# Ten expert blocks on chip instead of nine, gathered tokens and result rows in one buffer each, and a scatter by column halves

## The chip, the core and the metric

The kernel runs on one core of a Trainium2 chip. The metric is the device time of one execution in microseconds; lower is better. All work is float32. Engines are named as in the profile: PE (TensorE matmul), PEld (its weight loads), DVE (VectorE), ACT (ScalarE), POOL (GpSimd), SP (SyncE, which issues nearly all loads).

## What is computed

Two layers of a hybrid encoder block on 256 tokens of width 1024. Each layer has a mixer (one wide input projection, differential attention, a bidirectional state-space scan, gates, output projections) and then a hierarchical mixture of experts, in which each token goes to two of 32 experts:

```python
for i in range(DEPTH):                        # 2
    h = rms_norm(x, norm1_g[i])
    q, k, v, z, xbc, dt_raw, gate_a, gate_m = split(h @ w_in[i])
    ya = diff_attention(q, k, v, lam, rel_bias) @ w_attn_out[i]
    ym = ssd_mixer(z, xbc, dt_raw, ...) @ w_ssm_out[i]
    x = x + (sigmoid(gate_a) * ya + sigmoid(gate_m) * ym) @ w_out[i]
    hn = rms_norm(x, norm2_g[i])
    x = x + hier_moe(hn, ...)                 # top group of 4, top 2 of its 8 experts
# one expert: (silu(xb @ w_gate[e]) * (xb @ w_up[e])) @ w_down[e], 1024 -> 512 -> 1024
```

## The kernel before

Each engine has its own program; they meet at semaphores. A table of PSUM fills, `mixer_fills`, fixes in which order each of the eight PSUM banks is filled; `full`, `free`, `out_of` and `before` are waits on the counters of that table, `fill` and `drain` raise them.

**Mixer.** Weights come in 28 blocks of 2 MB through a ring of three slots (0 to 2). ACT copies each chunk of a block to a rounded high part (`cast`, L1324; four chunks of staging, `high`, in slot 3), POOL makes the low part (L2160), and PE multiplies in three products per tile (L791 to L793). SP issues the block loads in order (L645), each when the block three before it has been used (`BLOCK_USE`).

**Expert pass** (`first_pass`). All 32 experts are computed in 16 pairs; each expert takes up to 64 tokens, so a pair fills the 128 columns or rows of the array, one expert per half. Expert weights are 96 blocks of 2 MB in each layer: per pair two gate, two up and two down blocks, in that order. They go through nine slots (`slot_at`), in the order `ORDER`; load n is issued when block n - SLOTS has been used (`used`, L622). The first nine loads are issued by hand in the last part of the mixer as the memory under each slot comes free; loads 9 to 12 go in quarters and halves (L631), and so do the last pair's up and down blocks. Slots overlap mixer buffers: slot 6 is `r_h` and `r_g`, slot 7 `r_bt`, slot 8 `r_q` and `r_k`, slot 3 the staging of the high parts.

For one pair j, PE does: gate product g and up product u (L1185, 32 records of 7 us each), the scatter of pair j-1 for the first token half (`scatter`, L1130 and L1131), part of the gather for the pair of pairs after (`gather`, L1145: half of the work in every pair), the transposes of the hidden units (L1199), the turned selection matrix G (L1205, L1207), the scatter of the second token half, and the down product y2 in two column halves (L1217). ACT does silu (L1595), the copy of the hidden units (L1602), the copy of G (L1608, L1612), and the high rows of the result (L1619); DVE does the product of gate and up (L2053), the adds into X (L2061) and the low rows (L2071). Gathered tokens have two buffers (`xgT2`), result rows two column halves each for high and low (`yeh`, `yel`). The scatter of pair j runs in pair j+1; that of the last pair stands at the end, and after it either the next layer's norm (ACT L1342) or the store of the output (SP L747).

## Time and profile before

| | us |
|---|---|
| median of three runs | 1781.48 |
| lowest and highest | 1781.36, 1782.14 |
| profiled execution | 1784.47 |
| its span, first to last instruction | 1782.5 |
| PE busy | 1696.4 (95%) |
| DVE, ACT, POOL busy | 743.6, 684.7, 667.8 |
| loads and stores | 528.47 MB, 296 GB/s over the span |
| first expert product, layer 0 and layer 1 | 447.65 and 1332.89 |

Busy is time with an instruction on the engine. A matmul's end is modelled, so short waits inside a run of matmuls do not show as idle; a wait that the profile can't put down to another engine's instruction is called "issue". A DMA has its issue on SP, 0.33 us, and a time to landing; what counts for the reader of a slot is the landing.

### The profile page before, as it was taken

The numbers are of one execution on the slowest core, as the hardware profiler recorded it, in microseconds if no ns is written. First come the engines' busy times: TensorE is split into PE (matmuls) and PEld (weight loads), VectorE is DVE, ScalarE is ACT, GpSimd is POOL, SyncE is SP. The second block draws the span as 40 slices with busy tenths as digits, with TensorE's granted clock in tenths as the row PEclk, the third lists the DMA queues.
The fourth block names the chain that finished last, engine by engine and source line by source line (L and its number), as shares of the span: only waits on it lengthen the run. The fifth ranks groups of instructions, "written<-read, shape, count | busy, mean of one in ns | idle before, by whom it ended". The sixth has DMA issues, their size and how long they took to land.

```text
span 1782.5 us, 23201 instructions
## 1 busy us (share of the span) xinstructions
PE 1696.4 (95%) x8978; PEld 1057.9 (59%) x8978; DVE 743.6 (42%) x1318; ACT 684.7 (38%) x1541; POOL 667.8 (37%) x536
## 2 busy tenths in 40 slices
PE   8999999999999998999999999999999999998988
PEld 5889877776434434343368898777764444343433
DVE  5728787634222222211166387867341122121212
ACT  4565787744211111111056667877441111111111
POOL 6888776884000000000067987778830000000000
PEclk9999999999999999999999999999999999999999
DMA  6554312466999999999944452215669999999997
GB/s 250 206 189 154 131 58 86 151 252 281 418 419 427 427 429 427 427 427 428 415 193 171 184 189 95 96 48 194 267 281 416 428 427 428 429 427 427 428 428 302
DMA packets 45795, 528.47 MB, mean 296 GB/s; under 512 B 4936, under 2 KB 7752, under 8 KB 14960
## 3 DMA queue, kind: packets, MB, share of 16 engines
q1 hardware_dynamic: 45648, 526.89, 72.0%
q8 instruction: 76, 1.25, 0.3%
q14 instruction: 39, 0.32, 0.1%
q0 software_dynamic: 32, 0.02, 0.0%
HBM read 525.82 MB, written 1.06 MB: 296 GB/s over the span
## 4 chain that ended last, share of the span: by engine, by line
PE 77%; DVE 15%; issue 4%; ACT 3%; POOL 0%; DMA 0%; SPq 0%; DVEq 0%; ACTq 0%
PE PS L1185 25%; PE PS L1217 13%; PE PS L791 8%; PE PS L793 7%; PE PS L792 7%; DVE view L1807 5%; PE PS L1145 3%; PE PS L1130 3%; PE PS L1131 2%; DVE view L1803 1%; PE PS L998 1%; DVE view L1995 1%; DVE view L2061 1%; ACT view L1436 1%; PE PS L779 1%
## 5 line engine op out<-in xcount | busy, mean ns | idle before, releaser
L2160 POOL TENSOR_TENSOR view<-view,view 128x512 fp32r<-128x512 f32 x448 | 579.4, 1319 | 574.3 <-DVE view L1709 477.6
L1185 PE MATMUL PS<-view,view 128*64 128x512 f32 x2048 | 456.7, 602 | 35.1 <-issue 34.5
L1185 PEld LDWEIGHTS PS<-view,view 128*64 128x64 f32 x2048 | 157.7, 139 | 328.4 <-issue 328.1
L1324 ACT ACTIVATE view<-view 128x512 fp32r<-128x512 f32 x448 | 273.4, 629 | 155.7 <-PE PS L793 145.6
L791 PE MATMUL PS<-view,view 128*128 128x512 f32 x704 | 285.9, 406 | 5.7 <-POOL view L2160 3.2
L792 PE MATMUL PS<-view,view 128*128 128x512 f32 x704 | 275.4, 391 | 0.0
L793 PE MATMUL PS<-view,view 128*128 128x512 f32 x704 | 275.4, 391 | 0.0
L1217 PE MATMUL PS<-view,stb 128*64 128x512 f32 x1024 | 226.8, 595 | 0.3
L2053 DVE TENSOR_TENSOR view<-PS,view 128x512 f32<-128x512 f32 x32 | 22.1, 692 | 421.7 <-PE PS L1185 421.7
L791 PEld LDWEIGHTS PS<-view,view 128*128 128x128 f32 x704 | 132.6, 188 | 35.4 <-issue 7.5
L1217 PEld LDWEIGHTS PS<-view,stb 128*64 128x64 f32 x1024 | 70.7, 137 | 139.3 <-issue 138.8
L793 PEld LDWEIGHTS PS<-view,view 128*128 128x128 f32 x704 | 132.6, 188 | 29.2
L792 PEld LDWEIGHTS PS<-view,view 128*128 128x128 f32 x704 | 132.9, 189 | 23.4
L1560 ACT ACTIVATE view<-PS,vcol 128x256 f32<-128x256 f32 x64 | 26.7, 472 | 281.6 <-PE PS L1145 265.0
L2071 DVE SCALAR_TENSOR_TENSOR view<-PS,gcol,view 128x512 fp32r<-128x512 f32 x64 | 48.0, 751 | 205.5 <-ACT view L1619 205.5
L1619 ACT ACTIVATE view<-PS,gcol 128x512 fp32r<-128x512 f32 x64 | 44.0, 687 | 182.3 <-PE PS L1217 182.1
L896 PE MATMUL PS<-view,view 128*128 128x256 f32 x384 | 112.0, 292 | 0.0
L897 PE MATMUL PS<-view,view 128*128 128x256 f32 x384 | 108.6, 283 | 0.0
L898 PE MATMUL PS<-view,view 128*128 128x256 f32 x384 | 108.5, 282 | 0.0
L1595 ACT ACTIVATE view<-PS 128x512 f32<-128x512 f32 x32 | 19.1, 597 | 199.1 <-PE PS L1185 199.1
L1807 DVE SCALAR_TENSOR_TENSOR view<-PS,vcol,view 128x254 f32<-128x254 f32 x192 | 92.7, 483 | 6.8
L2061 DVE TENSOR_TENSOR view<-PS,view 128x512 f32<-128x512 f32 x128 | 82.6, 684 | 11.1 <-PE PS L1131 10.5
(250 smaller groups left out, 2038.1 us busy)
## 6 DMA issues: line engine op xcount, KB each, us to landing
view<-in_w_exp_gate_dram SPq DMA_DIRECT2D x62, 2048.0 KB, 27.9
view<-in_w_exp_up_dram SPq DMA_DIRECT2D x58, 2048.0 KB, 28.4
view<-in_w_mix_dram SPq DMA_DIRECT2D x56, 2048.0 KB, 7.8
view<-in_w_exp_down_dram SPq DMA_DIRECT2D x56, 2048.0 KB, 30.4
view<-in_w_exp_up_dram SPq DMA_DIRECT2D x24, 512.0 KB, 23.7
view<-in_w_exp_down_dram SPq DMA_DIRECT2D x24, 512.0 KB, 14.5
view<-in_w_exp_down_dram SPq DMA_DIRECT2D x4, 1024.0 KB, 10.6
view<-in_w_exp_gate_dram SPq DMA_DIRECT2D x4, 1024.0 KB, 13.0
```

Source lines behind the costliest of these rows:

```text
L791: pe.matmul(o, xh[:, k, ts], highs(chunk), start=(k == 0), stop=False)
L792: pe.matmul(o, xh[:, k, ts], weights(low8, chunk), start=False, stop=False)
L793: ins = pe.matmul(o, xl[:, k, ts], highs(chunk), start=False, stop=(k == last))
L896: pe.matmul(o, wh[:, i, :], hTh[:, k, :], start=(k == 0), stop=False)
L897: pe.matmul(o, wh[:, i, :], hTl[:, k, :], start=False, stop=False)
L898: ins = pe.matmul(o, wl[:, i, :], hTh[:, k, :], start=False, stop=(k == KD - 1))
L1185: ins = pe.matmul(bank(ph, name, j)[e * CAP:(e + 1) * CAP, :], xgT2[h % 2][:, k, at + e * CAP:at + (e + 1) * CAP], slot8[expert_block(j, k ...
L1217: ins = pe.matmul(PS[e * CAP:(e + 1) * CAP, 3 + n, :], hhT[:, k, e * CAP:(e + 1) * CAP], slot4[expert_block(j, 2, e)[1]][:, k, n * COLS:(n ...
L1324: nc.scalar.activation(highs(chunk), weights(slot8, chunk), ACT.Copy).then_inc(*high_ready.up(ph))
L1807: ins = v.scalar_tensor_tensor(out=a[:, lo:hi], in0=x_[:, lo + o:hi + o], scalar=w(j), in1=a[:, lo:hi], op0=ALU.mult, op1=ALU.add)
L2061: v.tensor_tensor(x_, bank(ph, "s", j, t, n), x_, ALU.add).then_inc(*drain(ph, "s", j, t, n))
L2160: g_.tensor_tensor(weights(low8, chunk), weights(slot8, chunk), highs(chunk), ALU.subtract).then_inc(*low_ready.up(ph))
```

## The change

- SLOTS goes from 9 to 10 with a new ORDER. The tenth slot is made of three pieces of memory (2048, 1024 and 1024 words of each partition), so a load of it is three DMAs.
- The room: gathered tokens get one buffer (`xgT1`), result rows one column half each for high and low (`yh`, `yl`; the very last half has a buffer of its own, `yh_end`, `yl_end`). Several mixer buffers move, and the high parts of the last mixer blocks are staged in `high2`.
- SP issues the first expert loads earlier and in another order: one after the scan, two around the gates, then one after another with the merging products; all ten before the expert pass. Two mixer blocks are loaded when their slot's own block has been used, not one block later. The next layer's first three mixer blocks wait for the second-last down product; the dt weights (`step_weights`) wait for the last scatter.
- The scatter goes by column halves (`put_back`): half 0 of pair j-1 after g of pair j, half 1 after u. The gather for the next two pairs stands wholly in odd pairs, in four parts. In the last pair both scatters and G stand between g and u.

```diff
-SLOTS = 9
+SLOTS = 10
 RING = 3
-ORDER = (4, 5, 1, 2, 7, 8, 0, 3, 6)
+ORDER = (7, 3, 6, 4, 5, 8, 1, 2, 0, 9)
+PIECES = ((0, 2048), (2048, 1024), (3072, 1024))
...
 def gathered(j):
 
-    return (2 * (j % 2), 2 * (j % 2) + 1) if j // 2 + 1 < HALVES else ()
+    return j % 2 == 1 and j // 2 + 1 < HALVES
...
-        f += [(("g", j), 0), (("u", j), 1)]
+        f.append((("g", j), 0))
         if j:
-            f += [(("s", j - 1, 0, n), 5 + n) for n in range(2)]
-        f += [(("xg", j // 2 + 1, i), 4 if i % 2 else 7) for i in gathered(j)]
+            f += [(("s", j - 1, t, 0), 5 + t) for t in range(TT)]
+        if j == ALL_PAIRS - 1:
+            f.append((("G", j), 7))
+            f += [(("s", j - 1, t, 1), 5 + t) for t in range(TT)]
+            f.append((("u", j), 1))
+        else:
+            f.append((("u", j), 1))
+            if j:
+                f += [(("s", j - 1, t, 1), 5 + t) for t in range(TT)]
+        if gathered(j):
+            f.append((("xg", j // 2 + 1, 0), 0))
         f.append((("hh", j), 2))
-        if j:
-            f += [(("s", j - 1, 1, n), 5 + n) for n in range(2)]
-        f.append((("G", j), 7))
-        f += [(("y2", j, n), 3 + n) for n in range(2)]
-    f += [(("s", ALL_PAIRS - 1, t, n), 5 + n) for t in range(TT) for n in range(2)]
+        if j < ALL_PAIRS - 1:
+            f.append((("G", j), 7))
+        if gathered(j):
+            f.append((("xg", j // 2 + 1, 1), 1))
+        f.append((("y2", j, 0), 3))
+        if gathered(j):
+            f.append((("xg", j // 2 + 1, 2), 7))
+        f.append((("y2", j, 1), 4))
+        if gathered(j):
+            f.append((("xg", j // 2 + 1, 3), 2))
+    f += [(("s", ALL_PAIRS - 1, t, 0), 5 + t) for t in range(TT)]
+    f += [(("s", ALL_PAIRS - 1, t, 1), t) for t in range(TT)]
...
+        xgT1 = view(r_x, KD, HALF)
+        yh, yl = (view(r_v + i * COLS, COLS, dt=F32R) for i in range(2))
+        yh_end, yl_end = (view(r_x + i * COLS, COLS, dt=F32R) for i in range(2))
...
-        sga, sgm = ([view(r + o, TT, COLS) for r in (r_g, r_w)] for o in (0, 1024))
-        junk = view(r_v, 2 * D)
+        ga0, gm0 = (view(r_g + i * 1024, TT, COLS) for i in range(2))
+        sga, sgm = ([view(r + n * 1024, TT, COLS) for n in range(2)] for r in (r_v, r_w))
+        junk = view(r_q, 2 * D)
...
-        S2 = [view(r, TT, HALF, dt=F32R) for r in (r_cbt + TT * P, r_rt)]
+        high2 = view(r_cbt, HIGHS, COLS, dt=F32R)
+        pieces = (r_x + 2 * D, r_v + D, r_cbt)
...
-            h = high[:, chunk % HIGHS, :]
+            h = (high2 if chunk >= REST + HIGHS else high)[:, chunk % HIGHS, :]
...
+                    if slot == SLOTS - 1:
+                        for to, (at, width) in zip(piece4 if kind == 2 else piece8, PIECES):
+                            sp.dma_start(to.rearrange("p k f -> p (k f)"), src.rearrange("a p f -> p (a f)")[:, at:at + width]
+                                         ).then_inc(*loaded[slot].up(ph))
+                        return
...
-                        sp.wait_ge(*filled[0 if i else 1].at(ph, 0))
+                        if l:
+                            sp.wait_ge(*filled[4].at(ph, -1))
+                    elif i - RING in (FB + 5, FB + 7):
+                        sp.wait_ge(*chunk_used.at(ph, CHUNK_USE[(i - RING + 1) * CHUNKS - 1]))
                     else:
                         sp.wait_ge(*full(ph, *BLOCK_USE[i - RING]))
                     sp.dma_start(slot8[i % RING].rearrange("p k c -> p (k c)"), src).then_inc(*loaded[i % RING].up(ph))
                     if l == 0 and i == RING - 1:
                         vectors(0, ph)
+                        step_weights(0, ph)
+                    if l and i == RING - 1:
+
+                        sp.wait_ge(*full(Phase(l - 1), "s", ALL_PAIRS - 1, 1, 1))
+                        step_weights(l, ph)
                     if i == RING + 1:
 
                         sp.wait_ge(*filled[4].at(ph, 0))
                         sp.wait_ge(s_skew, 16)
                         sp.dma_start(BT, bass.AP(table_dram.tensor, 0, [[1, P], [WIN, HEADS], [1, 384]])
                                      ).then_inc(*bt_in.up(ph))
+                    if i == FB + 5:
+
+                        sp.wait_ge(*out_of(ph, "sc", ATT - 1))
+                        sp.wait_ge(*full(ph, "y", UNITS_SCAN - 1))
+                        load(0, 0, 0)
                     if i == FB + 7:
+
+                        sp.wait_ge(*full(ph, "gm", 1, 1))
+                        load(0, 0, 1)
+                        sp.wait_ge(*gate_ready.at(ph, 2))
+                        load(0, 1, 0)
+                    if i == FB + 8:
 
                         sp.wait_ge(*full(ph, "mT", XT - 1))
                         sp.wait_ge(*sumsq.at(ph, 13))
-                        load(0, 0, 0)
+                        load(0, 1, 1)
                     if i == FB + 11:
 
                         sp.wait_ge(*full(ph, "ws", 1, 1))
-                        load(0, 0, 1)
                         load(0, 2, 0)
                 sp.wait_ge(*full(ph, "wa", 1, 1))
-                load(0, 1, 0)
-                sp.wait_ge(*full(ph, "wo", 0, 1))
-                load(0, 1, 1)
-                sp.wait_ge(*full(ph, "wo", 1, 1))
                 load(0, 2, 1)
                 load(1, 0, 0)
+                sp.wait_ge(*full(ph, "wo", 0, 1))
                 load(1, 0, 1)
-                sp.wait_ge(*full(ph, "lgT"))
+                sp.wait_ge(*full(ph, "wo", 1, 1))
                 load(1, 1, 0)
+                load(1, 1, 1)
...
+            def put_back(ph, j, n):
+
+                high_rows, low_rows = (yh_end, yl_end) if j == ALL_PAIRS - 1 and n else (yh, yl)
+                pe.wait_ge(*out_of(ph, "y2", j, n))
+                if n == 0:
+                    pe.wait_ge(*out_of(ph, "G", j))
+                for t in range(TT):
+                    pe.wait_ge(*free(ph, "s", j, t, n))
+                    o, pick_t = bank(ph, "s", j, t, n), Gm[:, t * P:(t + 1) * P]
+                    pe.matmul(o, pick_t, high_rows, start=True, stop=False)
+                    pe.matmul(o, pick_t, low_rows, start=False, stop=True).then_inc(*fill(ph, "s", j, t, n))
...
+                        if kind == 0:
+                            if j:
+                                put_back(ph, j - 1, 0)
+                            if j == ALL_PAIRS - 1:
+                                turned_selection(j)
+                                put_back(ph, j - 1, 1)
+                    if 0 < j < ALL_PAIRS - 1:
+                        put_back(ph, j - 1, 1)
+                    if gathered(j):
+                        gather(h + 1, 0)
                     pe.wait_ge(*out_of(ph, "u", j))
                     pe.wait_ge(*free(ph, "hh", j))
                     for k in range(FF // P):
                         ins = pe.transpose(PS[:, 2, k * P:(k + 1) * P], hh[:, k * P:(k + 1) * P], ident[:, :])
                     ins.then_inc(*fill(ph, "hh", j))
-                    if j == 0:
-                        pe.wait_ge(*gw_ready.at(ph, 1))
-                    pe.wait_ge(*free(ph, "G", j))
-                    for t in range(TT):
-                        pe.transpose(PS[:, 7, t * P:(t + 1) * P], S2[h % 2][:, t, at:at + P].bitcast(F32), ident[:, :])
-                    for t in range(TT):
-                        ins = pe.matmul(PS[:, 7, TT * P:TT * P + 2], S2[h % 2][:, t, at:at + P].bitcast(F32),
-                                        gw[:, t, 2 * j:2 * j + 2],
-                                        start=(t == 0), stop=(t == TT - 1))
-                    ins.then_inc(*fill(ph, "G", j))
-                    if j:
-                        scatter(ph, j - 1, 1)
+                    if j < ALL_PAIRS - 1:
+                        turned_selection(j)
+                    if gathered(j):
+                        gather(h + 1, 1)
                     pe.wait_ge(*out_of(ph, "hh", j))
...
+                                gather(h + 1, 2 + n)
...
-                for t in range(TT):
-                    scatter(ph, ALL_PAIRS - 1, t)
+                for n in range(2):
+                    put_back(ph, ALL_PAIRS - 1, n)
...
-                    for i in gathered(j):
-                        if i % 2 == 0:
-                            gathered_out(j // 2 + 1, i)
-                    rest(ph, j)
+                    if j:
+                        high_rows(ph, j - 1, 1)
+                    if j == ALL_PAIRS - 1:
+                        selection_out(ph, j)
+                    hidden_out(ph, j)
+                    if j < ALL_PAIRS - 1:
+                        selection_out(ph, j)
+                    if gathered(j):
+                        gathered_out(j // 2 + 1, 0)
+                    high_rows(ph, j, 0)
+                    if gathered(j):
+                        gathered_out(j // 2 + 1, 2)
                     if j == 2:
                         act.wait_ge(*flag_ready.at(ph, 1))
                         act.sem_inc(s_anchor, 1)
                         over = act.value_load(flag[0:1, 0:1], min_val=0, max_val=1)
+                high_rows(ph, ALL_PAIRS - 1, 1)
...
+            def high_rows(ph, j, n):
+
+                act.wait_ge(*full(ph, "y2", j, n))
+                end = j == ALL_PAIRS - 1 and n
+                if n and not end:
+                    act.wait_ge(*full(ph, "s", j, 1, 0))
+                elif j and not end:
+                    act.wait_ge(*full(ph, "s", j - 1, 1, 1))
+                nc.scalar.activation(yh_end if end else yh, PS[:, 3 + n, :], ACT.Copy, scale=gcol[:, 0:1]
+                                     ).then_inc(*yeh_ready.up(ph))
...
+                    if j:
+                        low_rows(ph, j - 1, 1)
+                        add(ph, j - 1, 0)
                     if j % 2 == 0 and j // 2 + 1 < HALVES:
                         select(j // 2 + 1)
+                    if j == ALL_PAIRS - 1:
+                        add(ph, j - 1, 1)
                     gated(ph, j)
-                    for i in gathered(j):
-                        if i % 2:
-                            gathered_out(j // 2 + 1, i)
-                    if j:
-                        add(ph, j - 1)
-                    scaled_low(ph, j)
+                    if 0 < j < ALL_PAIRS - 1:
+                        add(ph, j - 1, 1)
+                    if gathered(j):
+                        gathered_out(j // 2 + 1, 1)
+                    low_rows(ph, j, 0)
+                    if gathered(j):
+                        gathered_out(j // 2 + 1, 3)
                     if j == 2:
                         dve.wait_ge(*flag_ready.at(ph, 1))
                         dve.sem_inc(s_anchor, 1)
                         over = dve.value_load(flag[0:1, 0:1], min_val=0, max_val=1)
                     if j == ALL_PAIRS // 2 and l + 1 < DEPTH:
                         head_scales(Phase(l + 1))
-                add(ph, ALL_PAIRS - 1)
+                low_rows(ph, ALL_PAIRS - 1, 1)
+                for n in range(2):
+                    add(ph, ALL_PAIRS - 1, n)
```

## Rows read from the trace of the kernel before

**Rows 1.** Page, part 2: what the DMA engines moved in each fortieth of the span

```profile
GB/s 250 206 189 154 131 58 86 151 252 281 418 419 427 427 429 427 427 427 428 415 193 171 184 189 95 96 48 194 267 281 416 428 427 428 429 427 427 428 428 302
```

**Rows 2.** Windows, layer 0: us, busy per engine, clock, DMA share, GB/s; second: 512 KB loads

```profile
540.00:580.00 40.00, 38.68 (x200) 17.67 (x200) 10.57 (x19) 7.42 (x17) 0.00 (x0) 1.00 1.01 428
...
872.00:877.00 5.00, 5.00 (x26) 1.73 (x24) 0.00 (x0) 0.60 (x1) 0.00 (x0) 1.00 1.03 410
```

**Rows 3.** Timeline of PE: start, us, work; layer 0 to pair 2, layer 1 start

```profile
447.65 13.96 PE L1185 MATMUL PS<-view,view 128*64 128x512 f32 x64 [0.30 <-ACT view L1560]
461.53 2.17 PE L1145 MATMUL PS<-view,view 128*128 128x256 f32 x16
...
471.75 13.90 PE L1185 MATMUL PS<-view,view 128*64 128x512 f32 x64
...
490.34 0.47 PE L1130 MATMUL PS<-view,view 128*128 128x512 f32 x1 [0.66 <-DVE view L2061]
...
498.49 13.90 PE L1185 MATMUL PS<-view,view 128*64 128x512 f32 x64
...
1332.89 13.95 PE L1185 MATMUL PS<-view,view 128*64 128x512 f32 x64 [0.31 <-ACT view L1560]
```

**Rows 4.** Timeline of SP's DMA issues, layer 0: start, us from first to last issue

```profile
353.92 28.93 SPq L645 DMA_DIRECT2D view<-in_w_mix_dram  x4
...
431.74 0.33 SPq L622 DMA_DIRECT2D view<-in_w_exp_down_dram  x1
...
449.62 0.33 SPq L631 DMA_DIRECT2D view<-in_w_exp_up_dram  x1
...
472.33 6.82 SPq L622 DMA_DIRECT2D view<-in_w_exp_up_dram  x2
```

**Rows 5.** DMA view, us to landing, issued 417.45, 471.96, 472.33, 838.36, 1357.20

```profile
view<-in_w_exp_up_dram SPq DMA_DIRECT2D x1, 2048.0 KB, 7.7
...
view<-in_w_exp_gate_dram SPq DMA_DIRECT2D x1, 2048.0 KB, 9.1
...
view<-in_w_exp_up_dram SPq DMA_DIRECT2D x1, 2048.0 KB, 13.6
...
view<-in_w_exp_gate_dram SPq DMA_DIRECT2D x1, 2048.0 KB, 28.7
...
view<-in_w_exp_gate_dram SPq DMA_DIRECT2D x1, 2048.0 KB, 8.5
```

**Rows 6.** Timeline of PE, late pairs: products behind a wait; last two: last pairs

```profile
730.12 8.78 PE L1185 MATMUL PS<-view,view 128*64 128x512 f32 x32 [2.41 <-issue]
...
847.58 7.09 PE L1185 MATMUL PS<-view,view 128*64 128x512 f32 x32 [2.40 <-issue]
...
867.18 15.60 PE L1185 MATMUL PS<-view,view 128*64 128x512 f32 x64 [2.34 <-issue]
...
1749.90 13.95 PE L1185 MATMUL PS<-view,view 128*64 128x512 f32 x64 [0.64 <-issue]
```

**Rows 7.** Timeline of all engines, layer 0, behind the last pair's up product

```profile
882.82 0.69 DVE L2053 TENSOR_TENSOR view<-PS,view 128x512 f32<-128x512 f32 x1 [16.39 <-PE PS L1185]
...
884.39 0.60 ACT L1602 ACTIVATE stb<-PS 128x512 f32<-128x512 f32 x1 [7.84 <-PE PS L1199]
...
885.89 7.09 PE L1217 MATMUL PS<-view,stb 128*64 128x512 f32 x32
...
892.23 1.49 ACT L1619 ACTIVATE view<-PS,gcol 128x512 fp32r<-128x512 f32 x2 [5.57 <-PE PS L1217]
...
893.05 1.52 DVE L2071 SCALAR_TENSOR_TENSOR view<-PS,gcol,view 128x512 fp32r<-128x512 f32 x2 [6.23 <-ACT view L1619]
...
893.85 0.50 PE L1130 MATMUL PS<-view,view 128*128 128x512 f32 x1 [0.88 <-DVE view L2071]
...
894.62 3.03 DVE L2061 TENSOR_TENSOR view<-PS,view 128x512 f32<-128x512 f32 x4
```

**Rows 8.** Timeline of PE in the mixer of layer 0, second scan projection

```profile
364.21 0.44 PE L779 MATMUL PS<-ident,view 128*128 128x128 f32 x2 [2.52 <-DVE view L1700]
```

More of the change, by code:

```diff
@@ L407, in encoder @@
         small = sb("small", [P, 48])
[L408 removed]
         dtv, av, nac, eac, dend = (dtm[:, i] for i in range(5))
+        piece8 = [view(at, n // COLS, COLS) for at, (_, n) in zip(pieces, PIECES)]
+        piece4 = [view(at, n // D, D) for at, (_, n) in zip(pieces, PIECES)]
         ebias = av
@@ L1170, in first_pass, with turned_selection @@
                     first_gather(i, 1, XNl).then_inc(*fill(ph, "xg", 0, i))
+                def turned_selection(j):
+                    h, at = j // 2, (j % 2) * 2 * CAP
+                    if j == 0:
+                        pe.wait_ge(*gw_ready.at(ph, 1))
+                    pe.wait_ge(*free(ph, "G", j))
+                    for t in range(TT):
+                        pe.transpose(PS[:, 7, t * P:(t + 1) * P], S2[h % 2][:, t, at:at + P].bitcast(F32), ident[:, :])
+                    for t in range(TT):
+                        ins = pe.matmul(PS[:, 7, TT * P:TT * P + 2], S2[h % 2][:, t, at:at + P].bitcast(F32),
+                                        gw[:, t, 2 * j:2 * j + 2],
+                                        start=(t == 0), stop=(t == TT - 1))
+                    ins.then_inc(*fill(ph, "G", j))
                 for j in range(ALL_PAIRS):
@@ L1595, in gate, with hidden_out, selection_out @@
                 nc.scalar.activation(silug, PS[:, 0, :], ACT.Silu).then_inc(*drain(ph, "g", j))
+            def hidden_out(ph, j):
+                act.wait_ge(*full(ph, "hh", j))
+                act.wait_ge(*before(ph, "y2", j, 1))
+                nc.scalar.activation(hhT.rearrange("p k t -> p (k t)"), PS[:, 2, :], ACT.Copy
+                                     ).then_inc(*drain(ph, "hh", j))
+            def selection_out(ph, j):
+                act.wait_ge(*full(ph, "G", j))
+                if j:
+                    act.wait_ge(*full(ph, "s", j - 1, 1, 1))
+                act.wait_ge(*free(ph, "y2", j, 1))
+                nc.scalar.activation(Gm, PS[:, 7, 0:TT * P], ACT.Copy)
+                for e in range(2):
+                    rows = slice(e * CAP, (e + 1) * CAP)
+                    ins = nc.scalar.activation(gcol[rows, :], PS[rows, 7, TT * P + e:TT * P + e + 1], ACT.Copy)
+                ins.then_inc(*drain(ph, "G", j))
+                act.wait_ge(*out_of(ph, "G", j))
+            def high_rows(ph, j, n):
[4 more added lines that the diff above has]
+                elif j and not end:
+                    act.wait_ge(*full(ph, "s", j - 1, 1, 1))
+                nc.scalar.activation(yh_end if end else yh, PS[:, 3 + n, :], ACT.Copy, scale=gcol[:, 0:1]
+                                     ).then_inc(*yeh_ready.up(ph))
             def rest(ph, j):
-                yeh_done = yeh_ready if ph.unit is None else over_yeh[ph.layer]
                 act.wait_ge(*full(ph, "hh", j))
@@ L2053, in gated, with add, low_rows @@
                 v.tensor_tensor(hh, PS[:, 1, :], silug, ALU.mult).then_inc(*drain(ph, "u", j))
-            def add(ph, j):
+            def add(ph, j, n):
                 for t in range(TT):
-                    for n in range(2):
-                        x_ = X[:, t, n * COLS:(n + 1) * COLS]
-                        dve.wait_ge(*full(ph, "s", j, t, n))
-                        v.tensor_tensor(x_, bank(ph, "s", j, t, n), x_, ALU.add
-                                        ).then_inc(*drain(ph, "s", j, t, n))
+                    x_ = X[:, t, n * COLS:(n + 1) * COLS]
+                    dve.wait_ge(*full(ph, "s", j, t, n))
+                    v.tensor_tensor(x_, bank(ph, "s", j, t, n), x_, ALU.add
+                                    ).then_inc(*drain(ph, "s", j, t, n))
+            def low_rows(ph, j, n):
+                end = j == ALL_PAIRS - 1 and n
+                dve.wait_ge(*out_of(ph, "G", j))
+                dve.wait_ge(*yeh_ready.at(ph, 2 * j + n + 1))
+                v.scalar_tensor_tensor(out=yl_end if end else yl, in0=PS[:, 3 + n, :], scalar=gcol[:, 0:1],
+                                       in1=yh_end if end else yh, op0=ALU.mult, op1=ALU.subtract
+                                       ).then_inc(*drain(ph, "y2", j, n))
             def scaled_low(ph, j):
-                yeh_done = yeh_ready if ph.unit is None else over_yeh[ph.layer]
                 dve.wait_ge(*out_of(ph, "G", j))
```

93 lines of the change are left out of this document (52 added, 41 removed).

## Prediction

> **What bounds the kernel now.** I read the page's 40 slices first. From slice 11 to 19 and again from 31 to 39 the load rate stands at 418 to 429 GB/s, while the mixer before each stretch moves 58 to 281 GB/s [rows 1]. Those stretches are the expert passes: 96 loads of 2.10 MB in each layer. A window inside one says the same with the shares: PE 38.7 of 40 us, DMA share 1.01, 428 GB/s [rows 2]. At that rate one load takes 4.9 us and a pair of experts, six loads, 29.4 us. The timeline of PE gives the other side: pair 1 starts at 471.75 and pair 2 at 498.49 [rows 3], 26.7 us later and with no load waited for. So PE is faster than the queue, uses up its lead of nine slots and then has to wait. The late pairs show it: a wait of 2.3 to 2.4 us ahead of a product, named "issue", which is where a load lands [rows 6]. The landing of the second gate block of the last pair proves the tie: issued at 838.36, it lands 28.7 us later, at 867.06 [rows 5], and PE starts at 867.18 [rows 6]. In layer 1 the same product starts at 1749.90. So each layer is: time at which the last pair's gate blocks land, and then a chain of PE, ACT and DVE to the end. Both terms are changed here, with opposite signs.
>
> **Loads ahead: the gain.** Before, five loads are out when the last merging product ends; the other four of the nine slots are issued at 431.74 and after [rows 4]. After, eight of ten are out by then, and two more leave at once: 9.8 us plus about 2.8 us of latency (a lone load takes 7.7 us [rows 5], against 4.9 in the stream), so all ten are in by about 444, ahead of the first expert product at 447.65 [rows 3]. That empties the queue until the first quarter is released at 449.62 [rows 4], so three more slots are not worth three times 4.9 us. What counts is when load 14 (counted from 0, second load of the group released by pair 0's down product) lands. Before: issued 472.33, 13.6 us, so 485.9, or 38.3 us after the start of the expert pass [rows 3, 4, 5]. After: pair 0's down product ends earlier, because the gather between up and down (2.17 us [rows 3]) moves to pair 1. The gap from up to down, 24.1 less two products of 7.0 and one of 6.9, was 3.3 us with the gather in it and becomes 2.25 (the chain through the hidden units, worked out below), so that product ends at 23.0 us instead of 24.1. Load 14 is the first that it releases, the quarters ahead of it (four loads from 2.0 us on, 20 us) are just through, so it lands as a lone load, 7.7 us on, at 30.7 us. Lead: 7.6 us. In layer 1 the load before it is issued at 1357.20 and lands 8.5 us on, 32.8 us after that layer's start at 1332.89, where layer 0 needs 33.4 [rows 3, 5]; lead 7.0. From there both kernels run at the queue's rate and the lead stays: 14.6 us together. Ends: one slot each, 9.8; and 17 us if the queue keeps going.
> The cover for the lead is queue depth. Pair 1's down product releases the next loads at 49.2 us (23.0 + 7.0 gate + 0.9 + 7.0 up + about 11.3 for scatter, two gathers, hidden units, selection and down), and load 19 lands at 30.7 + 5 x 4.9 = 55.2, so 6 us of work remains and a gap needs less than 2.8.
>
> **Three pieces for slot 9: a cost.** Half of the tenth slot is loaded in pieces with rows of 4 KB. Where such loads run alone the window gives 410 GB/s against 428 [rows 2]: 1.05 MB takes 2.56 instead of 2.45 us. The 8 KB half has no row; I bound it between nothing and the same. Eight loads a layer behind the lead: 0.9 to 1.8 us, taken 1.3, twice 2.6.
> The Trainium skill (DMA: Bandwidth & Descriptors, "Anatomy of one DMA") gives each DMA a fixed part of about 2.0 us, and its "Bandwidth" section asks for 1 MiB and more per DMA; 16 further DMAs a layer would by that, as an estimate, be 32 us. The trace does not agree where loads queue: the window of 512 KB loads holds 410 GB/s. It is a rival below.
>
> **The last pair: a cost.** Before, its gate and up products run back to back, 13.95 us [rows 6], and scatters, selection and hidden units fill the 3.1 us from up to down: VectorE multiplies from 882.82, ACT copies the hidden units from 884.39 for 0.60, down starts at 885.89 [rows 7]. After, two scatters and the selection stand between gate and up. The second scatter needs rows that ACT scales only when the first scatter has read the one buffer. From the end E of the gate product: first scatter's second bank full at about E+1.2 (four matmuls of 0.22, and 0.77 from a bank's first matmul to the add that reads it [rows 7]); ACT, then VectorE 0.82 later, at E+2.05; its 0.76 and two adds of 0.76 free the banks at E+3.6 and E+4.3; the last two matmuls put up at about E+4.7. That is against 0 before. From up to down only the chain is left: 0.1 + 0.69 + 0.1, transposes, ACT 0.64 later for 0.60, about 2.25 instead of 3.15. Net +3.8; nothing hides it, since the up blocks land 9.8 us after the gate blocks and up now starts at 11.7. Ends +2.0 (if the scatter waits for nothing) and +4; I take 3.6, twice 7.2.
> **The end.** Scatters by column halves leave the four adds (3.03 us from 894.62 [rows 7]) as the bound, so the end stays; but a token half is whole only after three adds, not two. Layer 1's first square starts 0.76 later, and as the second has to wait for it the cost is 0.55. At the end of the kernel two stores are issued together: +0.2.
>
> **Costed at nothing.** Within the other pairs a wait for the adds of 0.66 goes [rows 3] and the gathers are laid together in odd pairs; the queue is the bound there, so it is idle PE time moved. ACT's and VectorE's new waits (the second half's rows wait for the first scatter) stand in front of the hidden units, but end about 4.2 us after the gate product, inside the up product's 7.0. If that cover were gone, each pair would pay the excess up to the 2.4 us of idle [rows 6]. The next layer's first three mixer loads leave earlier than the end of the last up product, but they queue behind the same tail loads, and their first reader is the cast behind the next norm; nothing gained, nothing lost. The dt weights now wait on SyncE for the last scatter; behind them stands only the fourth mixer load, which waits for a product of the new layer anyway, and their own cast comes after a whole mixer block. In the mixer SyncE waits for the end of the scan and for ACT's gates, each with an expert load behind it and then mixer loads. The mixer load behind the gates went out at 353.92 [rows 4], when a whole projection was done; now it goes after the first half, some 12 us earlier, with two expert loads of 4.9 us ahead of it, so it lands no later than before (353.92 and 8.5). The same holds for the block two further on. The one PE wait there, 2.52 us [rows 8], ends with VectorE's work and not with a load. I take 0, ends -2 and +2 over both layers.
>
> **Sum.** -14.6 + 2.6 + 7.2 + 0.75 = -4.05 us. The profiled execution took 1784.47 (span 1782.5), so it would be 1780.4; it is 3.0 over the median of 1781.48, from which the forecast is 1777.4.
>
> **Rivals.** (B) The detour in the last pair costs 2.0 a layer and the lead is 8: -16 + 2.6 + 4.0 + 0.75 = -8.65, 1772.8; with the mixer's 2 us, 1770.8. For it: PE could find the banks free, if adds are seen quicker than I set them. Chance 0.27.
> (C) Not what it says: the lead is one slot, 4.9 a layer, since the queue stands empty ahead of the first release. -9.8 + 10.55 = +0.75, 1782.2. For it: the idle stretch from 444 to 449.6. Against it: load 14's time counts, not load 9's. Chance 0.18.
> (D) Slower: the deeper buffer starves. A release that comes when the queue is drained costs 7.7 - 4.9 = 2.8 us. If pair 1's release and two more come late in each layer, 8.4 us a layer, the lead is gone: +16.8 - 4.05 = 1794.2. It decides at pair 1's release: later than 52.4 us after the start, where I have 49.2. PE's clock is its smaller form: of the waits of 2.3 to 2.4 us some are followed by a product that is 1.7 us longer (8.78 against 7.09, 15.60 against 13.95) and some are not [rows 6]; four more on the ends of layers would give 1784.2, five go past 1785. Chance 0.09.
> (E) Every piece pays a fixed part, the 2.8 us of a lone load: 16 x 2.8 = 45 us a layer, 1869. The window at 410 GB/s speaks against it. Chance 0.02.
> The forecast itself 0.44, own range 1774.5 to 1780.5.
>
> **Chances.** A measurement of this kernel tells about 0.2%, 3.6 us, from no change: 1777.9 and 1785.0 are the bounds. Faster: B and a good half of the forecast, 0.51. Same: the rest of it and C, 0.38. Slower: D and E, 0.11. The range leaves out E, most of D and the edge of B: 1770.8 to 1785.
>
> **What would show it.** Right: the first expert product finds all ten slots landed; last gate landing 7 us nearer to the start of the expert pass; a step of about 4.7 us between the last pair's gate and up products; down 2.25 after up; rate 425 GB/s or more in the stretch with three-piece loads. Wrong: gaps in the load rate 20 to 60 us into the pass; waits ahead of up products gone altogether (then PE is the bound, and its shorter pairs count); PE waits for casts in the mixer.

## The result, and the profile after

| | before | after |
|---|---|---|
| median of 14 runs, us | 1782.36 (1781.17 to 1784.26) | 1787.01 (1782.73 to 1790.84) |
| ratio to before | | 1.0024, interval 1.0017 to 1.0031 |
| profiled execution, us (span) | 1784.47 (1782.5) | 1786.88 (1784.9) |
| granted clock, mean | 0.994 | 0.993 |

The changed kernel is 4.65 us slower by the medians, 4.3 by the ratio (interval 3.0 to 5.5); I had forecast 4 us faster and a time under 1785.0. Its runs also spread over 8.1 us, those of before over 3.1. The two profiled executions differ by only 2.4 us in span: before's lay above the highest of its 14 timed runs, after's near its median. The steps below account for those 2.4 us; the other 2.2 of the medians' difference are not located.

The page first: what the DMA engines moved in each fortieth of the span, to be laid beside [rows 1].

```profile
GB/s 251 204 188 159 126 65 125 298 221 236 364 416 426 427 426 426 427 426 426 419 154 166 175 181 95 95 115 309 226 228 414 428 426 425 426 427 426 427 425 221
```

The plateau is the same, 425 to 428. The last slice falls from 302 to 221 and the one behind the first pass from 193 to 154: the loads are done earlier and PE goes on longer without them. The lead was gained, and something behind it grew.

PE's timeline of after (start, us, work, idle time before it and what ended it), as in [rows 3, 6]: first expert products of each layer, and the last pair's gate, up and down products.

```profile
447.41 7.09 PE L1277 MATMUL PS<-view,view 128*64 128x512 f32 x32 [0.30 <-ACT view L1655]
...
862.00 8.78 PE L1277 MATMUL PS<-view,view 128*64 128x512 f32 x32 [2.60 <-issue]
...
875.46 7.09 PE L1277 MATMUL PS<-view,view 128*64 128x512 f32 x32
...
884.74 7.09 PE L1307 MATMUL PS<-view,stb 128*64 128x512 f32 x32 [0.73 <-ACT stb L1705]
...
1331.46 7.09 PE L1277 MATMUL PS<-view,view 128*64 128x512 f32 x32 [0.30 <-ACT view L1655]
...
1743.89 8.78 PE L1277 MATMUL PS<-view,view 128*64 128x512 f32 x32 [2.57 <-issue]
...
1757.35 8.79 PE L1277 MATMUL PS<-view,view 128*64 128x512 f32 x32
...
1768.32 7.09 PE L1307 MATMUL PS<-view,stb 128*64 128x512 f32 x32 [0.73 <-ACT stb L1705]
```

Measured from each layer's first expert product, the last pair's gate product starts at 414.6 and 412.4 us; before it was 419.5 and 417.0 [rows 3, 6]. So the net lead is 4.9 and 4.6 us, not the 6.3 and 5.7 that 7.6 and 7.0 less the pieces would give. From that product's start to the down product it is 22.7 and 24.4 us, where the kernel before took 18.7 and 17.0. That is 11.4 us more over both layers. Part of it is in the durations: three of the four gate and up products last 8.8 us in place of 7.1, where before has one such (15.60 in place of 13.95 for the two together [rows 6]). That is 3.4 us; the other 8.0 are the detour.

Where the lead fell short is in the windows of after (us, busy time of each engine, clock, DMA share, GB/s):

```profile
445.00:450.00 5.00, 4.70 (x30) 3.00 (x30) 2.78 (x12) 3.52 (x8) 0.00 (x0) 1.00 0.00 0
450.00:455.00 5.00, 5.00 (x26) 2.08 (x24) 2.04 (x9) 1.37 (x2) 0.00 (x0) 1.00 0.80 265
...
470.00:475.00 5.00, 5.00 (x26) 1.71 (x24) 0.00 (x0) 0.00 (x0) 0.00 (x0) 1.00 0.96 385
```

All ten slots are full and the queue stands still, as I had said; then it does not start at 427 GB/s but at 265. The 20 us that I gave to the quarters released from 2.0 us on became longer: load 14, issued at 470.62, finds the queue still at work and lands 9.6 us on (forecast 7.7, a lone load), at 480.2, which is 32.8 us after the start of the pass (forecast 30.7, before 38.3). From a lead of 5.5 there, 0.6 more goes by the end of the pass.

All engines of after between the last pair's gate and up products, layer 0:

```profile
870.72 0.50 PE L1209 MATMUL PS<-view,view 128*128 128x512 f32 x1
...
872.00 0.69 ACT L1729 ACTIVATE view<-PS,gcol 128x512 fp32r<-128x512 f32 x1 [0.58 <-PE PS L1210]
872.79 0.75 DVE L2204 SCALAR_TENSOR_TENSOR view<-PS,gcol,view 128x512 fp32r<-128x512 f32 x1 [15.20 <-ACT view L1729]
873.46 1.28 DVE L2196 TENSOR_TENSOR view<-PS,view 128x512 f32<-128x512 f32 x2
...
874.29 0.47 PE L1209 MATMUL PS<-view,view 128*128 128x512 f32 x1 [1.82 <-DVE view L2196]
```

This is the step as it was worked out: first scatter, ACT, VectorE, second scatter, and the up product at 875.46, 4.7 us after the gate product's end. PE waits 1.82 us in it.

### The profile page after: what moved, and what is told of

It is laid out like the page before. It is cut to its first block, busy times and chain, and to the rows that moved or that the text cites. A ratio compares the mean times of both kernels' runs of the same rounds, so it can differ in the third digit from the quotient of the medians.

```text
span 1784.9 us, 23220 instructions
## 1 busy us (share of the span) xinstructions
PE 1706.5 (96%) x8978; PEld 1059.4 (59%) x8978; DVE 741.7 (42%) x1318; ACT 683.2 (38%) x1541; POOL 667.4 (37%) x536
## 4 chain that ended last, share of the span: by engine, by line
PE 65%; DMA 14%; DVE 13%; ACT 4%; issue 4%; SPq 0%; POOL 0%; DVEq 0%; ACTq 0%
PE PS L1277 18%; DMA view<-in_w_exp_down_dram 14%; PE PS L1307 10%; PE PS L857 8%; PE PS L859 7%; PE PS L858 7%; DVE view L1933 5%; PE PS L1223 2%; PE PS L1209 1%; DVE view L1929 1%; PE PS L1064 1%; ACT view L1531 1%; PE PS L1210 1%; PE PS L845 1%; DVE stat L1807 1%
## 5 line engine op out<-in xcount | busy, mean ns | idle before, releaser
L1705 ACT ACTIVATE stb<-PS 128x512 f32<-128x512 f32 x32 | 19.1, 598 | 276.9 <-PE PS L1297 259.4
```

## Experiments

Each ratio is to the kernel before, run beside it on the same chip, with its 95% interval in brackets; the medians of the kernel before were then 1782.62 to 1783.89 us. First the detour of the last pair was undone.

**1. The last pair as all others.** In the changed kernel:

```diff
-                            if j == ALL_PAIRS - 1:
+                            if j == ALL_PAIRS:
                                 turned_selection(j)
                                 put_back(ph, j - 1, 1)
-                    if 0 < j < ALL_PAIRS - 1:
+                    if 0 < j < ALL_PAIRS:
                         put_back(ph, j - 1, 1)
```

and the same bound in the plan of the banks, on ACT and on VectorE.

> The changed kernel with one thing undone: in the last pair the second scatter and the turned selection stand where they stand in every other pair (scatter of the second column half after the up product, selection after the transposes of the hidden units). Theory 1 (the detour between the last gate and up products is what made the change slower): the step from gate to up, 13.5 us in the trace of the changed kernel, falls to about 8.0; the gap from up to down grows from 2.3 to about 3.3. Net 3.8 us less in each layer, and the idle stretch in which the clock could fall goes too: 1787.0 - 7.6 - 1 to 3 = 1776 to 1778. Rival (the buffers shared by all pairs cost it, the detour is worth only its own matmuls, 2.1 a layer): 1783 or more.

Measured: 1778.53 us (1777.21 to 1780.22), ratio 0.9972 [0.9961, 0.9984]. PE's timeline of this kernel:

```profile
860.67 8.78 PE L1277 MATMUL PS<-view,view 128*64 128x512 f32 x32 [2.56 <-issue]
...
870.52 7.09 PE L1277 MATMUL PS<-view,view 128*64 128x512 f32 x32
...
879.88 7.09 PE L1307 MATMUL PS<-view,stb 128*64 128x512 f32 x32
```

Gate to down is 19.2 us, 17.5 with the 1.7 of the slow gate product taken off; in after it is 22.7 or 21.05, before 18.7 or 17.04. The detour therefore costs 3.5 us a layer against this order and 4.0 against the kernel before. The two ratios differ by 0.52%, 9.3 us, where two steps of 3.5 make 7.0; the intervals allow 6 to 12 us, so that the difference holds the 7.0. The median lies just above the 1776 to 1778 of theory 1 and far below the rival's 1783. Both traces have four stretches of slow products on the path (table in 5), so in the traces the clock does not make the difference.

**2. The clock.** Ten dummy products were put ahead of the last pair's gate product and seven into the gap of the detour, in banks that are written next anyway:

```diff
+                        if kind == 0 and j == ALL_PAIRS - 1:
+                            pe.wait_ge(*free(ph, name, j))
+                            dummies(0, 10)
...
+                                pe.wait_ge(*free(ph, "u", j))
+                                dummies(1, 7)
```

> The changed kernel with idle PE time filled: 10 dummy matmuls of 0.22 us ahead of the wait for the last pair's gate blocks (a wait of 2.6 us), 7 between the turned selection and the second scatter (a wait of 1.8 us). Theory (the spread of the changed kernel, 1782.7 to 1790.8, is products of the last pairs run at half the granted clock, 1.7 us each, some two a run over before): no product of the last pairs over 7.1 us, mean clock 0.995 or 0.996, median 1783 to 1784, spread 2 us or less. Rival (the spread is something else, and dummies only take time): 1787 to 1789 with the same spread.

Measured: 1783.63 us (1781.83 to 1787.15), ratio 1.0002 [0.9992, 1.0011]. All four last gate and up products take 7.09 us in its trace, in after one of four does:

```profile
862.28 7.09 PE L1286 MATMUL PS<-view,view 128*64 128x512 f32 x32 [0.29 <-issue]
...
874.04 7.09 PE L1286 MATMUL PS<-view,view 128*64 128x512 f32 x32
...
1744.36 7.09 PE L1286 MATMUL PS<-view,view 128*64 128x512 f32 x32 [0.33 <-issue]
...
1756.12 7.09 PE L1286 MATMUL PS<-view,view 128*64 128x512 f32 x32
```

It is 3.4 us faster than after by the medians and 3.9 by the ratios, and the two intervals do not meet. So the waits around the detour do cost clock as well. In the traces three stretches of slow products go and a new one stands near 1250 us, which is two fewer, 3.4 us. The spread was not cured: it is 5.3 us against the 2 that I expected, and one of its ten runs took 1787.15.

**3. The pieces.** Three more slots of the changed kernel load in three pieces, 4 of 10 in place of 1:

```diff
-    if n % SLOTS == SLOTS - 1:
+    if n % SLOTS in (5, 6, 7, SLOTS - 1):
```

> The changed kernel with the loads of three more slots cut in three DMAs as the tenth slot's are (29 or so more loads in pieces in each layer). Queue theory (pieces cost only through their 4 KB rows, 0.08 to 0.2 us a load, in a queue that is the bound): +2 to +5 us a layer, 1791 to 1797. Rival 1 (each piece has a fixed part of its own, 2.0 to 2.8 us, which a queue doesn't hide): 1787 + 2 x 56 x 2.0 = over 2000. Rival 2 (the queue is not the bound): 1787.

Measured: 1793.67 us (1790.69 to 1797.07), ratio 1.0065 [1.0048, 1.0082], 0.41% over after, as expected. The last gate products start 3.2 and 4.1 us later in their pass than in after. The trace has 27 more loads in pieces a layer; 3.7 us for them is 0.14 us each. The windows agree: this kernel, then after.

```profile
540.00:600.00 60.00, 59.87 (x304) 26.52 (x304) 13.43 (x24) 10.15 (x25) 0.00 (x0) 1.00 1.01 422
```

```profile
540.00:600.00 60.00, 59.87 (x305) 26.54 (x304) 13.28 (x24) 10.33 (x25) 0.00 (x0) 1.00 1.00 425
```

0.7% of 60 us is 0.42 us, for some 3.7 more loads in pieces. At 0.14 us the change's own eight behind the lead cost, as an estimate, 1.1 a layer (I took 1.3). The Trainium skill (DMA: Bandwidth & Descriptors, "Anatomy of one DMA") gives a fixed part of about 2.0 us for each DMA, fitted to DMAs issued from GpSimd; here SyncE issues them. It does not add up where loads queue: these 54 further DMAs a layer would by that, as an estimate, cost over 100 us, and 3.7 were measured.

**4. The tenth block late.** In the changed kernel the tenth block is loaded only behind the first released quarter, so that nine are ahead:

```diff
-                load(1, 1, 1)
...
+                    if part == 0:
+                        load(1, 1, 1)
```

> The changed kernel with the tenth block not loaded ahead: its load is issued when the first quarter of a gate block is released, 2 us into the expert pass. Theory (the end of each layer follows the landing of the last pair's gate blocks, and a block that lands ahead of the pass is worth 4.9 us): +4.9 us a layer less at most 1 us because the emptied queue starts earlier with large rows, 1795 to 1797. Rival (PE's own sum is the bound of the changed kernel, so that a lead is worth nothing): 1787.

Measured: 1792.21 us (1790.31 to 1793.03), ratio 1.0047 [1.003, 1.0064], under the 1795 to 1797 that I expected. The last gate product starts 417.5 and 416.2 us into its pass, 2.9 and 3.7 later than in after. Its windows:

```profile
445.00:450.00 5.00, 4.70 (x30) 2.88 (x30) 2.75 (x13) 3.81 (x8) 0.00 (x0) 1.00 0.00 0
450.00:455.00 5.00, 5.00 (x26) 2.03 (x24) 1.78 (x8) 1.22 (x2) 0.00 (x0) 1.00 0.94 312
...
470.00:475.00 5.00, 5.00 (x26) 1.72 (x24) 0.00 (x0) 0.00 (x0) 0.00 (x0) 1.00 1.01 419
```

One more load in the queue brings the restart from 265 to 312 GB/s and fills the dip at 470 (385 to 419). So a block ahead is worth 3 to 4 us rather than the 4.9 of its transfer, because with it the queue is emptier when the first releases come. The forecast of the lead had left this out; whether it is all that it lacked, this run does not tell.

**5. Last pair undone, with ten dummies ahead of the gate product.** The edit of 1 and the first half of the edit of 2.

> The changed kernel with the last pair's scatter and selection back in their places (as in the first experiment, 1778.5 against 1783.9 for the kernel before in the same session) and 10 dummy matmuls ahead of the wait for the last pair's gate blocks. Clock theory (in that experiment's trace the last gate product of layer 0 took 8.78 us behind a wait of 2.6 us, that of layer 1 7.09): no last gate product over 7.1 us, 1 to 2.5 us less, 1776 to 1777.5, ratio to the kernel before 0.996. Rival (the half clock comes at random whatever PE did before): 1778.5.

Measured: 1776.48 us (1775.04 to 1779.1), ratio 0.9969 [0.9958, 0.9981], as expected, and faster than both kernels. To the kernel of 2 it is 7.15 us by the medians and 5.9 by the ratios, where two steps of 3.5 make 7.0. To kernel 1, whose one difference is the dummies, it is 2.05 us by the medians but 0.5 by the ratios, so their gain is not shown by this pair. From the steps of its trace I would have it faster still. Where the rest is shows in layer 1's mixer. PE's timeline there: of this kernel, then of after.

```profile
1245.60 0.53 PE L851 MATMUL PS<-ident,view 128*128 128x128 f32 x2 [2.52 <-DVE view L1835]
1245.79 0.76 PE L863 MATMUL PS<-view,view 128*128 128x512 f32 x1
1246.35 0.63 PE L864 MATMUL PS<-view,view 128*128 128x512 f32 x1
```

```profile
1249.72 0.44 PE L845 MATMUL PS<-ident,view 128*128 128x128 f32 x2 [2.52 <-DVE view L1826]
1249.92 0.48 PE L857 MATMUL PS<-view,view 128*128 128x512 f32 x1
1250.23 0.39 PE L858 MATMUL PS<-view,view 128*128 128x512 f32 x1
```

The same wait of 2.52 us, the same products, and behind it the half clock in one execution and the full one in the other. I then looked for every stretch with a granted clock under 1 in all traces, by windows of 3 us. The clock is at 0.5 in them (1.2 of 2.4 GHz), and they come in one size, 1.71 us lost each (kernel 9 has two end to end near 699). A stretch inside an expert pass is taken in by the waits for loads behind it: in before the slow product at 1730.30 is followed by a wait of 0.64 ahead of the last gate product, where it is 2.3 in layer 0. The others are on the path:

| kernel | half clock on the path, near (us) | in the passes |
|---|---|---|
| before | 363, 867 | 4 |
| after | 363, 861, 1743, 1755 | 2 |
| 1 | 363, 861, 897, 1245 | 2 |
| 2 | 363, 1248 | 2 |
| 3 | 363, 864 | 4 |
| 4 | 363, 864, 1749, 1761 | 4 |
| 5 | 363, 897, 1245 | 4 |
| 6 | 363, 1251 | 5 |
| 7 | 363, 1248 | 5 |
| 8 | none | 3 |
| 9 | none | 5 |

(and one at the end of each kernel).

**6. The detour alone, on the kernel before.** Scatter, selection, scatter between gate and up of the last pair, with the double buffers of before:

```diff
+                        if kind == 0 and j == ALL_PAIRS - 1:
+                            scatter(ph, j - 1, 0)
+                            turned_selection(j)
+                            scatter(ph, j - 1, 1)
```

> The kernel before (nine slots, double buffers) with the detour alone: in the last pair both scatters and the selection stand between the gate and the up product. Theory (with two buffers the second scatter waits for nothing, so the detour costs the work of PE between gate and up, 2.9 us, less the 0.9 that the up-to-down gap shrinks by; the other 1.8 a layer of the changed kernel come from the single result buffer): +2.0 a layer, 4 us over the kernel before, 1787.6 where that is 1783.6. Rival 1 (the detour costs 3.8 with any buffers): +7.6, 1791. Rival 2 (the work is hidden by the landing of the up blocks): no difference.

Measured: 1788.13 us (1787.33 to 1790.04), ratio 1.0034 [1.0019, 1.0048]. The last pair in its trace:

```profile
866.42 7.09 PE L1199 MATMUL PS<-view,view 128*64 128x512 f32 x32 [2.32 <-issue]
...
876.28 7.09 PE L1199 MATMUL PS<-view,view 128*64 128x512 f32 x32
...
885.50 7.09 PE L1227 MATMUL PS<-view,stb 128*64 128x512 f32 x32 [0.69 <-ACT stb L1612]
```

Gate to down 19.08 us against 17.04: 2.04 a layer, 4.1 in all, is the order; the other 2.0 a layer in after fit the wait of 1.82 for the one buffer of result rows. These two parts were not told apart in the forecast except as its ends. The ratio gives 6.1 us, and its interval (3.4 to 8.6) holds the 4.1. The waits ahead of both last gate products are as long as before's (2.32 and 2.31), yet neither product is slow.

**7. Dummies ahead of the last gate product of the kernel before.**

> The kernel before with 10 dummy matmuls ahead of the wait for the last pair's gate blocks. Clock theory: in its trace the last gate product of layer 0 had 1.7 us of half clock behind a wait of 2.3 us and that of layer 1 none, so between 0 and 1.7 us less in the median and nothing that depends on the double buffers: 1782 to 1783 where the kernel before is 1783.6. Rival (the clock doesn't matter before, only behind the detour): 1783.6.

Measured: 1784.83 us (1781.22 to 1787.36), ratio 1.0009 [1.0, 1.0019]; a miss, for I had expected 1782 to 1783. The half clock at 867 is gone (gate and up together 13.95 us, not 15.60), but in layer 1 there was hardly a wait to fill:

```profile
1749.09 2.33 PE L772 MATMUL PS<-maskb,identb 128*128 128x512 bf16 x10
1751.36 1.08 PE L1194 MATMUL PS<-view,view 128*64 128x512 f32 x4
```

The gate product starts 418.6 us into its pass, before 417.0, where it had waited 0.64 [rows 6]. The dummies stood in its way by what they gained in layer 0, and the mixer of layer 1 had a half-clock stretch at 1248 that before had not.

**8 and 9. All waits bridged,** on kernel 5 and on kernel 7: ten dummies more at the wait of 2.52 us [rows 8] and more products in the bridge, the products on constants with which PE passes the time between the layers: `bridge(9)` in kernel 8, as shown, and `bridge(7)` in kernel 9.

```diff
+                    if h == 4:
+                        pe.wait_ge(*free(ph, "wa", 0, 0))
+                        dummies(0, 10)
...
-                    bridge(6)
+                    bridge(9)
```

> The kernel of e5 (last pair undone, ten dummy products ahead of the last gate product) with dummies at two further waits of PE, the only ones outside the expert passes behind which traces show a half-clock stretch: ten ahead of the fifth transpose of the map outputs (wait 2.52 us in both layers; half clock behind it in layer 0 in all nine profiles, in layer 1 in five of them), and three more products in the bridge between the layers (wait 1.75 us; half clock behind it in e5 and in the kernel with the last pair undone). Nothing of the kernel's own work is left out. Each half-clock stretch in the traces costs 1.7 us. Theory 1 (the gain of the deeper buffer, 9 to 10 us by the steps of the traces against 5.5 in the medians, is partly returned in such stretches on the path): the stretches at 363, 897 and 1245 us go, and the median is 3.4 to 5 us under e5's 1776.5, about 1772. Theory 2 (the clock falls anyway, at another place, as it did in layer 1's mixer when the last gate product's wait of the kernel before was filled): 1775 to 1777. Theory 3 (the dummies sit in the way of the next work): over 1777.

> The kernel before with the same three kinds of dummies (ten ahead of the last gate product, ten at the wait of 2.52 us in the mixer, one more bridge product where the wait between the layers is 0.90 us). Theory 1: the stretches at 363 and 1248 us go; against 1784.8 with the last dummies alone, 1781.5 to 1783, that is within 1 us of the kernel before; and the difference between this kernel and e8 is then the deeper buffer's own worth with no half clock in it, 8.5 to 10 us. Theory 2: 1784 to 1785.5, and the difference to e8 stays at 7.6 to 8.3.

Measured: 1775.76 us (1774.9 to 1778.7), ratio 0.9964 [0.9951, 0.9977], and 1784.23 us (1783.09 to 1786.56), ratio 1.0009 [1.0, 1.0019]. Neither trace has a half-clock stretch on the path. Windows of kernel 8, at the places where kernel 5 has a clock of 0.83, 0.88 and 0.83:

```profile
360.00:370.00 10.00, 8.53 (x43) 5.95 (x42) 6.32 (x13) 4.09 (x8) 5.05 (x5) 1.00 0.09 39
...
890.00:900.00 10.00, 9.43 (x33) 5.09 (x32) 5.37 (x20) 5.50 (x12) 4.04 (x4) 1.00 0.48 193
1240.00:1250.00 10.00, 8.53 (x43) 5.91 (x42) 6.61 (x12) 3.90 (x8) 5.05 (x5) 1.00 0.12 51
```

Yet kernel 8 is not the 1772 that I expected; the times of theory 2 came (1775 to 1777 and 1784 to 1785.5), though not its reason, a clock that falls elsewhere; the difference of the pair, 8.5, is at the lower end of theory 1. Kernel 8's timeline says why:

```profile
363.18 2.33 PE L838 MATMUL PS<-maskb,identb 128*128 128x512 bf16 x10 [1.47 <-DVE view L2033]
```

The bank for the dummies comes free only 1.47 us into the wait of 2.52, and 1.47 + 2.33 is 1.3 us longer than the wait, in both layers. So 2.6 us were paid for a clock that in kernel 5 had cost up to 5.1 (three stretches). The gain measured is 0.7 by the medians; it would fit if not every run has all three. What is clean is the difference of the pair, 8.5 us by the medians and 0.45%, 8.0 us, by the ratios, with no half clock on the path of either trace: the change without its detour is worth 8 to 8.5 us (the intervals of the ratios allow 4 to 12). The two traces sum to the same. The lead is 5.7 and 4.8 us; from it go 0.44 in each layer between gate and down and 0.9 for a longer end, while a first pass that starts 0.8 later and a mixer 0.8 shorter cancel. That makes 8.6, the difference of the spans.

## Why the prediction was wrong, point by point

Two terms of the sum failed. "Loads ahead" was too large by 2.5 us, because load 14 was taken to land alone; the slow products of PE behind a wait stood at nothing in the sum and took 3.4. A third failing is behind the sum: the 3.0 us carried from the profile to the median.

- **What bounds the kernel**: right. Both kernels reach the last gate product when its load lands (waits of 2.60 and 2.57 in after, 2.34 and 0.64 in before), and the rate in the pass is 425 to 428 GB/s. Two readings of [rows 1] were off without effect: the 31st slice has 416, not 418, and the mixer's lowest 48, not 58.
- **Loads ahead, 7.6 and 7.0 us**: right in kind, too large in size. Load 14 landed at 32.8 and not at 30.7 us. The failed step is "the quarters ahead of it (four loads from 2.0 us on, 20 us) are just through": they restart an idle queue at 265 GB/s. Experiment 4 shows that link by moving one load into the gap. Load 14 left nearly when it should, at 23.2 us for 23.0 (24.1 less 20.9 is 3.2 and not 3.3, which gives 23.1). Net of the pieces the lead was 4.9 and 4.6 instead of 6.3 and 5.7, 2.5 us over both layers. The 9.5 us of both layers lie midway between the forecast's 12.0 and the 7.2 of rival C, and in part for C's reason.
- **Pieces, 1.3 a layer**: near. 0.14 us a load by experiment 3, about 1.1 a layer. In after only 0.6 us of lead goes behind load 14; what gives the rest back isn't known. The fixed part of rival E is refuted (whose 1869 adds up to 1867). No queue starved (D): pair 1's release came at 50.7 us (498.07), before the 52.4 of the limit, and from 465 to 505 us the DMA share is 1.00 at 418 GB/s.
- **The last pair, 3.6 a layer**: right. The up product starts 4.7 us behind the gate product, as worked out, and down 2.2 behind up. Measured 4.0 a layer, nearer to the 3.8 that was worked out than to the 3.6 taken. That "nothing hides it" held.
- **The end**: +0.55 in layer 0 was wrong in sign, -0.2 (17.08 to 16.89 from the down product's start to the next layer's first transposes); +0.2 in layer 1 was 1.0 in after's trace, where the kernel ends 16.6 us after its down product (before 15.6). The same code took 16.6 in kernel 1 too, but 15.0 in kernel 5. The last adds are done 0.7 us earlier than before; what differs is the stores behind them. I don't know what decides that.
- **Costed at nothing**: held. The new waits of ACT and VectorE in the other pairs are hidden, and layer 1's mixer takes 429.8 us against 429.9.
- **The clock**: the step that turned the sign in the traces (-4.05 with 2.5 and 0.8 added is still a gain). I had it as a small form of rival D, at 0.09 with the starving queue, although the rows showed products 1.7 us longer behind waits [rows 6], and the change moved PE's waits onto the path: a wait of 2.6 ahead of each last gate product (0.64 in layer 1 before) and a gap of 1.82 in the detour. After's trace has two such stretches on the path more than before's, 3.4 us; experiment 2 leaves two fewer and gets 3.4 to 3.9 back.
- **From the profile to the median**: I took off 3.0 us because before's profiled execution lay that far above its median. After's own lies 0.1 under its median. Of the 3.0, 0.9 was that the median of three runs lay under that of 14 (1782.36). The distance of a profile from the median belonged to that execution here and could not be carried over.

The 9.6 us between 1777.4 and 1787.0 are then: lead 2.5, detour 0.8 (8.0 in place of 7.2), clock 3.4, carried distance 3.1, and -0.2 for the rest.

What stays open: which of the waits of 1.8 to 2.6 us are followed by the half clock. Of the 11 unfilled waits of 2.3 to 2.6 us ahead of a last gate product, 7 were; of the six gaps of 1.82 in the detour, 2 (before, after, 1, 3, 4 and 6). Filling one removed it there each time, and in kernels 2, 6 and 7 a stretch stood near 1250 that neither before nor after had. Kernels 1 and 5 lie 5.4 and 6.1 us under before by the medians (5.0 and 5.5 by the ratios), 2 to 3.5 short of the clean pair's 8 to 8.5; the stretches at 897 and 1245 account for 3.4 us in their profiled executions, but how many of the timed runs have them isn't shown.

## What to carry to other kernels

A change that puts a new wait of PE on the path may pay for it twice: count such waits outside the queue-bound part, and give each a share of the 1.7 us of slow products as a likely cost (here 7 of 11 for waits of 2.3 to 2.6 us, 2 of 6 for 1.8), not as a tail. A deeper prefetch that runs full and lets the queue go idle is worth less than the transfer time of its extra block (here 3 to 4 us of 4.9), since the restart is slow. When a reorder on the last unit of work is made only to fit a smaller buffer, price that unit alone: here the order cost 2 and the single buffer another 2 us a layer, and leaving the last pair as it was gave 1778.5 in place of 1787.0 (1776.5 and 1775.8 with waits filled by dummies).

## What the runs showed of the hardware

The same wait with the same products behind it (2.52 us in layer 1's mixer) is followed by the full clock in before, after, 3 and 4 and by the half clock in 1, 2, 5, 6 and 7; in layer 0 all nine traces without dummies there have the half clock. In these traces each stretch costs 1.71 us, never part of it, but for the one in which the kernel ends. And small VectorE operations of 128x2 take 1.2 us while GpSimd works and 0.16 between its operations. They stand in the VectorE chain that ends this wait; that the wait would be shorter without GpSimd's work is likely from this, but no run shows it. All engines of kernel 5 ahead of the wait:

```profile
359.43 1.21 DVE L1817 SCALAR_TENSOR_TENSOR stat<-stat 128x2 f32<-128x2 f32 x1
...
360.68 0.16 DVE L1815 TENSOR_TENSOR stat<-stat 128x2 f32<-128x2 f32 x1
360.82 1.28 POOL L2313 TENSOR_TENSOR view<-view,view 128x512 fp32r<-128x512 f32 x1 [0.20 <-ACT view L1428]
...
360.87 1.24 DVE L1816 SCALAR_TENSOR_TENSOR stat<-stat 128x2 f32<-128x2 f32 x1
```
